# The second block's mixer: the values' and the latents' projections moved between the rounds of neighbourhood attention

## The reference

```
z = rms_norm(h, mix_pre_g) @ w_in                 # 512 x 1952
q_na, k_na, v_na, c_q, c_kv, k_rope = split(z)    # 512, 512, 512, 256, 128, 32 columns
o_na  = neighbourhood_attention(q_na, k_na, v_na, na_rpb)
o_mla = latent_attention(c_q, c_kv, k_rope, q_norm_g, w_uq, kv_norm_g, w_ukv, cos, sin)
mixed = concat(rms_norm(o_na), rms_norm(o_mla)) @ w_out
h = h + rms_norm(mixed, mix_post_g)
```

## Time and profile before

| | us |
|---|---|
| median of 3 runs | 1896.31 (1894.67 to 1901.78) |
| the profiled execution, its own time | 1902.84 |
| its span, first to last instruction | 1901.0 |
| TensorE busy | 1801.5 (95%) |
| VectorE busy | 962.7 (51%) |
| ScalarE busy | 853.9 (45%) |
| mean granted TensorE clock | 0.972 |

### The profile page before, as it was taken

How to read it: one execution, slowest core, us unless ns; L and a number is a source line. 1 busy time by engine, 2 the same in 40 slices (tenths; PEclk the granted TensorE clock), 3 DMA queues, 4 the chain that set the end, 5 groups by cost and what they waited for, 6 DMA issues and landing times.

```text
span 1901.0 us, 22849 instructions
## 1 busy us (share of the span) xinstructions
PE 1801.5 (95%) x8653; PEld 1424.6 (75%) x8653; DVE 962.7 (51%) x1528; ACT 853.9 (45%) x1336; POOL 261.1 (14%) x317
## 2 busy tenths in 40 slices
PE   8998999999779999989999999998899999999997
PEld 6886666667658888867888888776577678888886
DVE  3546344445369999965432343443656453323334
ACT  4236665552348888864222322323555442222222
POOL 4001532220001111120000000160223100000000
PEclk9998999999979999999999999999799999999998
DMA  7224011114469999673332333143101223223321
GB/s 212 86 73 133 24 41 49 45 45 155 177 257 359 385 384 388 260 239 106 92 107 81 108 91 109 60 137 91 51 12 54 58 78 99 100 88 101 98 101 56
DMA packets 161172, 246.59 MB, mean 130 GB/s; under 512 B 11346, under 2 KB 117041, under 8 KB 148144
## 3 DMA queue, kind: packets, MB, share of 16 engines
q1 hardware_dynamic: 152768, 232.57, 36.3%
q0 software_dynamic: 8304, 12.69, 2.2%
HBM read 239.42 MB, written 12.61 MB: 133 GB/s over the span
## 4 chain that ended last, share of the span: by engine, by line
PE 88%; DVE 6%; ACT 3%; issue 2%; DMA 1%; POOL 0%; DVEq 0%; SPq 0%; ACTq 0%
PE psum L472 25%; PE psum L474 25%; PE psum L473 24%; PE psum L624 3%; PE psum L652 3%; PE psum L608 3%; ACT warea_r L432 1%; PE psum L630 1%; PE psum L1353 1%; DVE xarea L2041 1%; DVE warea_r L438 1%; DVE xarea L2412 1%; DMA arena<-in_w_in 0%; ACT arena L1706 0%; DMA arena<-y_assigned 0%
## 5 line engine op out<-in xcount | busy, mean ns | idle before, releaser
L438 DVE TENSOR_TENSOR warea_r<-warea,warea_r 128x2048 fp32r<-128x2048 f32 x108 | 250.7, 2322 | 318.5 <-ACT warea_r L432 318.4
L472 PE MATMUL psum<-tarea_r,warea_r 128*128 128x512 f32 x916 | 366.0, 400 | 4.0 <-DVE tarea_r L2051 3.8
L474 PE MATMUL psum<-tarea_r,warea_r 128*128 128x512 f32 x916 | 359.1, 392 | 0.0
L473 PE MATMUL psum<-tarea_r,warea_r 128*128 128x512 f32 x916 | 359.0, 392 | 0.0
L472 PE MATMUL psum<-warea_r,arena_r 128*128 128x512 f32 (+1 forms) x768 | 300.3, 391 | 12.9 <-DVE warea_r L438 4.0
L432 ACT ACTIVATE warea_r<-warea 128x2048 fp32r<-128x2048 f32 x108 | 205.9, 1907 | 234.4 <-PE psum L474 231.9
L474 PE MATMUL psum<-warea_r,arena_r 128*128 128x512 f32 (+1 forms) x768 | 297.5, 387 | 0.0
L473 PE MATMUL psum<-warea_r,arena_r 128*128 128x512 f32 (+1 forms) x768 | 297.2, 387 | 0.0
L472 PEld LDWEIGHTS psum<-tarea_r,warea_r 128*128 128x128 f32 x916 | 173.2, 189 | 48.3 <-issue 10.0
L474 PEld LDWEIGHTS psum<-tarea_r,warea_r 128*128 128x128 f32 x916 | 173.3, 189 | 36.9
L473 PEld LDWEIGHTS psum<-tarea_r,warea_r 128*128 128x128 f32 x916 | 173.4, 189 | 34.7 <-issue 0.7
(11 more groups left out here) (329 smaller groups left out, 2465.8 us busy)
## 6 DMA issues: line engine op xcount, KB each, us to landing
warea<-in_ffn_w_gu SPq DMA_DIRECT2D x88, 512.0 KB, 5.0
warea<-in_w_in SPq DMA_DIRECT2D x40, 512.0 KB, 4.5
warea<-in_ffn_w_down SPq DMA_DIRECT2D x40, 512.0 KB, 4.2
arena<-in_w_up SPq DMA_DIRECT2D x16, 1024.0 KB, 7.4
tarea<-in_w_up SPq DMA_DIRECT2D x16, 1024.0 KB, 7.3
tarea<-in_w_down SPq DMA_DIRECT2D x16, 1024.0 KB, 7.7
warea<-in_w_gate SPq DMA_DIRECT2D x14, 1024.0 KB, 7.4
harea<-in_w_gate SPq DMA_DIRECT2D x14, 1024.0 KB, 7.9
```

Of the source, the lines that this page charges most:

```text
L438: dve.tensor_tensor(w_lo[:, u % 2, :], raw_of(u), w_hi[:, u % 2, :].bitcast(f32), ALU.subtract)\
L472: nc.tensor.matmul(out, high, by_high, start=first, stop=False)
L473: nc.tensor.matmul(out, high, by_low, start=False, stop=False)
L474: return nc.tensor.matmul(out, low, by_high, start=False, stop=last)
```

## The change

- Tables 0, 1 and 2 are made between the halves of the keys' block, into banks 0 to 2. Table 3 comes at the end of TensorE's round 0, tables 4 to 7 at the ends of rounds 6, 7, 9 and 10 (on VectorE at the starts of rounds 1, 7, 8, 10 and 11).
- The values' block is no longer ahead of the rounds: its first half is fill of rounds 0 (row blocks 0, 1) and 1 (2, 3), its second half of rounds 2 and 3, in banks 6, 4, 7, 5. The evacuations are in ScalarE's openings of rounds 3 and 4.
- The latents' block is fill of rounds 4 to 7 (row blocks 0 and 1 by halves, then 2, then 3), with evacuations in rounds 6 to 8.
- The splits of units 5, 6 and 7 move into the closings (ScalarE: 6 in round 1, 7 in round 3; VectorE: 0, 2 and 4). Pair 0's evacuation, unit 8's high part and the root are all in ScalarE's closing of round 8; VectorE's variance, evacuation and rotation in 8, unit 8's low part in 9, scaling in 9 and 10, the copy and unit 9's low part in 11.
- Turning in rounds 11 and 12, MLA jobs in 13 to 20, sums of squares in 21. The band transfers stand one unit earlier in SyncE's queue.

The diff, cut:

```diff
 MLA_AT = 4 * NT
+TABLE_ROUND = {1: (3,), 7: (4,), 8: (5,), 10: (6,), 11: (7,)}
...
 
+        if ph["name"] == "second":
+            yield from TABLE_ROUND.get(d, ())
...
-            if u is not None and ph["units"][u]["last_of_pair"]:
...
-        return [j for j in (2 * (d - 12), 2 * (d - 12) + 1) if 0 <= j < len(MLA_JOBS)]
...
             for u in range(AT_MID, AT_FFN2):
                 feed(u)
-                if u == AT_MID + 9:
+                if u == AT_MID + 8:
                     sp.wait_ge(s["z2_evac"], 4)
                     for b, band in enumerate((0, 8, 24, 32)):
                         for r in range(4):
                             src = v2[64 * (r % 2) + band:64 * (r % 2) + band + 32, :, :]
                             sp.dma_start(Vband[32 * r:32 * r + 32, b, :].rearrange("p (j n) -> p j n", j=2),
                                          src[:, r // 2:r // 2 + 3:2, :]).then_inc(s["band_in"], 16)
...
-            for n in range(3):
+            for n in range(2):
...
-                    if n == 2 and h == 0:
+                    if n == 1 and h == 0:
                         pe.wait_ge(s["xrev_in"], 16 * 8 * H)
+                        for g in range(3):
+                            pe.wait_ge(s["z2_first"], g + 1)
+                            na_table(g, ps[g])
+            pe.wait_ge(s["na_tab"], 3)
+            pe.wait_ge(s["z2_first"], 5)
+            def values(r, h):
+
+                u = AT_MID + 4 + h
                 if r == 0:
-                    for h in range(2):
-                        pe.wait_ge(s["split_lo"], AT_MID + 6 + h + 1)
-                else:
-                    pe.wait_ge(s["z2_evac"], 4 + r)
-                for k in range(KD):
-                    mm = products(ps[6][:, 0:416], hT_hi[:, k, P * r:P * r + P], hT_lo[:, k, P * r:P * r + P],
-                                  *weights(AT_MID + 6 + k // 4, 416 * (k % 4), 416), k == 0, k == KD - 1)
-                mm.then_inc(s["z2_psum"], 1)
+                    pe.wait_ge(s["split_lo"], u + 1)
+                if h == 0:
+                    if r < 2:
+                        pe.wait_ge(s["z2_first"], (7, 5)[r])
+                    else:
+                        pe.wait_ge(s["na_tab"], 4)
+                for c in range(4):
+                    k = 4 * h + c
+                    mm = products(ps[V_BANK[r]], hT_hi[:, k, P * r:P * r + P], hT_lo[:, k, P * r:P * r + P],
+                                  *weights(u, 512 * c, 512), k == 0, k == KD - 1)
+                if h:
+                    mm.then_inc(s["z2_psum"], 1)
+                elif r == NT - 1:
+                    mm.then_inc(s["unit_done"], 1)
+
+            def latent(r, h):
+
+                u = AT_MID + 6 + h
+                if r == 0:
+                    pe.wait_ge(s["split_lo"], u + 1)
+                if h == 0:
+                    pe.wait_ge(s["z2_evac"], (1, 3, 5, 7)[r])
+                for c in range(4):
+                    k = 4 * h + c
+                    mm = products(ps[7 if r == 1 else 6][:, 0:416], hT_hi[:, k, P * r:P * r + P], hT_lo[:, k, P * r:P * r + P],
+                                  *weights(u, 416 * c, 416), k == 0, k == KD - 1)
+                if h:
+                    mm.then_inc(s["z2_psum"], 1)
 
...
+                pe.wait_ge(s["cn_ready"], 5 if c == 3 else 4)
                 if c < 2:
-                    pe.wait_ge(s["cn_ready"], 5)
...
             def second_fill(d):
 
-                if 1 <= d <= 4:
-                    if d == 1:
-                        pe.wait_ge(s["na_tab"], 1)
-                    latent(d - 1)
-                if d in (10, 11):
-                    latent_turned(2 * (d - 10))
-                    latent_turned(2 * (d - 10) + 1)
+                if d < 4:
+                    for r in range(2 * (d % 2), 2 * (d % 2) + 2):
+                        values(r, d // 2)
+                for r, h in {4: ((0, 0), (1, 0)), 5: ((0, 1), (1, 1)), 6: ((2, 0), (2, 1)), 7: ((3, 0), (3, 1))}.get(d, ()):
+                    latent(r, h)
+                for g in tables_at(second, d + 1):
+                    if g == 3:
+                        pe.wait_ge(s["z2_first"], 8)
+                    if g == 4:
+                        pe.wait_ge(s["z2_evac"], 6)
+                    na_table(g)
+                if d in (11, 12):
+                    latent_turned(2 * (d - 11))
+                    latent_turned(2 * (d - 11) + 1)
                 for j in mla_jobs(d):
                     mla_job(j)
-                if d == 20:
+                if d == 21:
                     pe.wait_ge(*mla_evac(len(MLA_JOBS) - 1))
                     pe.wait_ge(*mla_evac(len(MLA_JOBS) - 2))
                     norm_sums(0)
                 if d in OUT_ROUND:
                     out_job(OUT_ROUND[d])
 
-            attend_pe(pe, second, na_table, second_fill)
+            attend_pe(pe, second, fill=second_fill)
...
-            for n in range(3):
+            for n in range(2):
                 split_high(AT_MID + 2 * n + 2)
                 if n == 0:
                     row_copy(3, ps[7])
-                for r in range(4 if n > 1 else 0):
-                    q = 4 * n + r
-                    act.wait_ge(s["z2_psum"], q + 1)
-                    nc.scalar.activation(v2[:, r, :], ps[q % 8], ACT.Identity, scale=late[3][:, r:r + 1]).then_inc(s["z2_evac"], 1)
                 split_high(AT_MID + 2 * n + 3)
 
             def second_opening(d):
 
-                if 2 <= d < 6:
-                    r = d - 2
+                for r in {3: (0, 1), 4: (2, 3)}.get(d, ()):
+                    act.wait_ge(s["z2_psum"], 8 + r + 1)
+                    nc.scalar.activation(v2[:, r, :], ps[V_BANK[r]], ACT.Identity, scale=late[3][:, r:r + 1])\
+                        .then_inc(s["z2_evac"], 1)
+                for r in {6: (0, 1), 7: (2,), 8: (3,)}.get(d, ()):
                     act.wait_ge(s["z2_psum"], 12 + r + 1)
-                    nc.scalar.activation(z3[:, r, :], ps[6][:, 0:416], ACT.Identity, scale=late[3][:, r:r + 1])\
+                    nc.scalar.activation(z3[:, r, :], ps[7 if r == 1 else 6][:, 0:416], ACT.Identity, scale=late[3][:, r:r + 1])\
                         .then_inc(s["z2_evac"], 1)
-                for c in {11: (0, 1), 12: (2, 3)}.get(d, ()):
+                for c in {12: (0, 1), 13: (2, 3)}.get(d, ()):
                     act.wait_ge(s["cn_psum"], c + 1)
                     nc.scalar.activation(krot if c == 3 else cT_hi[:, c, :], ps[6 + c % 2], ACT.Copy).then_inc(s["ct_ready"], 1)
                 for j in mla_jobs(d - 1):
...
             def second_closing(d):
 
-                if d == 5:
+                if d == 1:
+                    split_high(AT_MID + 6)
+                if d == 3:
+                    split_high(AT_MID + 7)
+                if d == 8:
+                    evac_high(0)
                     latent_high(AT_MID + 8, Q_PARTS)
-                if d == 6:
                     root(rstd[:, 16:24])
-                if d == 7:
+                if d == 10:
                     latent_high(AT_MID + 9, KV_PARTS)
-                if d == 21:
+                if d == 22:
                     root(rstd[:, 24:28])
-                if d in (20, 22, 27, 33):
-                    split_high(AT_MID + {20: 10, 22: 11, 27: 12, 33: 13}[d])
-
-            attend_act(act, second, pair_high(second, lambda pair: o2[pair // 4][0][:, pair % 4, :], 984),
-                       fill=second_opening, split=second_closing)
+                if d in (20, 23, 27, 33):
+                    split_high(AT_MID + {20: 10, 23: 11, 27: 12, 33: 13}[d])
+
+            evac_high = pair_high(second, lambda pair: o2[pair // 4][0][:, pair % 4, :], 984)
+            attend_act(act, second, evac_high, fill=second_opening, split=second_closing)
...
             for n in range(2):
                 split_low(AT_MID + 2 * n + 2)
                 if n == 0:
                     dve.wait_ge(s["row_ready"], 3)
+                else:
+                    dve.wait_ge(s["const_in"], 32)
+                    for g in range(3):
+                        na_table(g, ps[g])
                 for r in range(4):
...
-                split_low(AT_MID + 2 * n + 3)
-            split_low(AT_MID + 6)
-            split_low(AT_MID + 7)
+                if n == 0:
+                    split_low(AT_MID + 3)
...
-                for c in {11: (0, 1), 12: (2,)}.get(d, ()):
+                for c in {12: (0, 1), 13: (2,)}.get(d, ()):
...
             def second_closing(d):
 
-                if 2 <= d < 6:
-                    t = d - 2
+                for u in {0: (5,), 2: (6,), 4: (7,)}.get(d, ()):
+                    split_low(AT_MID + u)
+                for t in {6: (0, 1), 7: (2,), 8: (3,)}.get(d, ()):
                     dve.wait_ge(s["z2_evac"], 4 + t + 1)
                     for k, (a, b_) in enumerate(((0, 256), (256, 384))):
```

(46 more changed lines are left out.)

35 lines of the change are left out of this document (5 added, 30 removed).

## The result

The changed kernel took 1908.36 us (median of 6 runs, 1904.90 to 1913.62) against 1898.53 for the kernel before (6 runs, 1894.67 to 1901.78): ratio 1.0054 [1.0037, 1.0071]. It is slower by half a per cent, 12 us over the forecast of 1896 and outside its range. The profiled execution took 1906.38 with a span of 1904.5, 3.5 more than the span before; the stretch from round 22 to the end is 474.4 in both, so the difference arises ahead of it, as the prediction had it.

A forecast was written before the change was run, and what follows sets the result against it. It held TensorE to bound the stretch only while a projection lies beside the rounds, the VectorE-ScalarE loop bounding rounds 5 to 12. The gap's gain was given back at later waits: minus 0.1 us, so 1896, range 1886 to 1902.

The forecast's parts named there:

- Step 1: Keys' block: three tables add 1.9 us of TensorE; VectorE has time for its nine operations, 3.1 us.
- K: End of the keys' products, forecast at 1285.4 (1283.49 + 1.9); later times in the prediction are counted from it.
- Steps 2 to 5: Rounds 0 to 12: old gap gone, round 8 7.8 us earlier, then given back at waits; first MLA job at 91.4.
- Step 6: First MLA job to round 22: 49.7 us against 51.9 before, by minus 1.16 and minus 1.0; moved sums of squares nothing.
- The sum: Whole kernel: minus 0.1 us, span 1901.0 to 1900.9, median 1896.2, rounded 1896.
- A: First output product, round 5: no wait for the band transfers; minus 6 us, 1890; 15%.
- B: Rounds 8 to 12 run at 4.94 us each despite ScalarE's block; first job 6.1 earlier, 1890; 15%.
- C: TensorE's clock stays at half through rounds 13 and 14 after three gaps; plus 4.1 us, 1900; 15%.
- D: Rounds 0 to 3: each round's values wait and are not fill, showing as idle time; 2%, inside C's chance.
- that I don't see: An unnamed wait that, together with C, would make the kernel slower by 9.5 us; 6%.
- The rule weighed: ScalarE's table switches, end of round 8: skill's 2.66 each would give 1899; the forecast kept 1.30.

The follow-up runs named there:

- e1: Changed kernel with table 2 no longer waiting on TensorE for tables 0 and 1: 1898.10 us, ratio 0.9999 to the kernel before.
- e4: The changed kernel run again unaltered, as base of its group: 1906.42 us, ratio 1.0034 to the kernel before.
- e2: Kernel before with only tables 0 and 1 moved between the halves of the keys' block: 1897.45 us, ratio 0.9988.
- e7: e1 with value rows evacuated before the split, plus e5's and e6's edits and tables 6 and 7 a round earlier: 1893.82 us, ratio 0.9982.
- e10: e1 with value rows 2 and 3 evacuated before the split, plus the edits of e5 and e6: 1894.34 us, ratio 0.9968.
- e6: e1 with value rows evacuated before the split, and unit 8's high part moved to round 8's opening: 1892.93 us, ratio 0.9961.
- e9: Changed kernel, wait kept, with five idle matmuls (ten in the trace) before table 2: 1904.59 us, ratio 1.0027 to the kernel before.
- e5: e1 with value rows evacuated before the split, and GpSimd issuing half of the band transfers: 1894.82 us, ratio 0.9978.

## Why the prediction was wrong

**Step 1 failed.** All that made the stage longer than forecast lies in it. It priced three tables by their matmuls, 3 x 0.65 = 1.9, and asked only whether VectorE's nine operations would delay the keys' evacuation. It did not ask what `na_table` waits for: for table 2, the tables 0 and 1 as VectorE has them, and in VectorE's queue these stand behind the low part of a unit whose split begins when the keys' first half ends. The terms were in the rows: a split of 1.9 and table operations of 2.07 for six, a low part of 2.3 by the profile's page. Together 6.3; TensorE's own tables 0 and 1 fill 1.3 of it (2 x 0.65), so the wait would have come out at 5.0. I had even named VectorE's queue as the cause of the old gap, from the earlier trace rows, and did not carry that reading to the new place: the old gap's line of waits said what the moved call depends on. K was to be 24.56 after the row factor (1283.49 + 1.9 - 1260.83); without the wait it was 24.73 (e1), with it 31.48 and, in the second trace, 32.84. "Nothing" as the lower bound and 3.1 as the upper one were bounds of the wrong queue: VectorE's delay, not TensorE's wait.

**Steps 2 to 5 held,** counted from the first scores, 1291.19: first output product at 1335.11 behind a wait of 4.85 (I had 4.05) and at half clock for 3.31 (3.8); round 8 at +60.4 (59.4); second output product +68.9 (68.1; the forecast start of its idle time and its length gave the same place); table 7 +79.6 (79.5) behind 6.17 (6); first MLA job +91.4 (91.4). The last one is in part luck: the terms from 88.0 on, at most a bare round of 1.63, 0.6 and 0.65, add up to 90.9 and not to the 91.4 that I wrote. The band's transfers took 11.41 of SyncE, 0.85 more than in the earlier trace rows, and that is the longer wait.

**Step 6** was 2.1 long: from the first job to round 22 it is 47.6, not 49.7. The first twelve products of the jobs went at full clock; I had taken 1.0 for that, half of the clock's cost, and it was 1.8 (4.70 before, 2.94 now). The other 1.2 is the term that I put at nothing, what runs at half clock behind the sums of squares. Round 21 took 8.16 in the trace of the kernel before and 6.95 in that of e2, which has the same instructions there. One us in the scores of that round, before and then in e2:

```profile
1420.00:1421.00 1.00, 1.00 (x8) 0.84 (x6) 0.00 (x0) 1.00 (x2) 0.19 (x1) 0.50 0.00 0
```
```profile
1416.00:1417.00 1.00, 1.00 (x12) 0.91 (x10) 0.00 (x0) 1.00 (x2) 0.20 (x1) 1.00 0.00 0
```

The changed kernel had 1.00 from 1423 to 1429, over its sums and what follows them. So 1.2 of the 51.9 that I started from belonged to the one trace rather than to the program, as far as two traces tell, and that it made the stage's miss smaller is luck.

**The sum.** Step 1 cost 6.9 more than I had (31.48 less 24.56), the rest 2.2 less (138.9 from the first scores to round 22 against 141.1), so the stage would be 4.7 over my forecast, and the first traces show 4.6 over the stage before. The medians show more: 12.0 over the 1896.31 that the forecast started from. Of this, 2.2 is the median of the kernel before (1896.31 in three runs, 1898.53 in six), which leaves 9.8. Without the 1.2 of round 21 the two traces of the changed kernel are 5.8 and 8.1 over the stage before, and the second group of runs has the medians 6.8 apart (1906.42 in e4, 1899.64 before). What of the 9.8 lies beyond that is not shown; the runs scatter ahead of the stage by more.

**The rivals.** A (no wait for the band) fell with the 4.85; B (rounds 8 to 12 at 4.94 each) with round 13 at 1380.29, 28.7 behind round 8; C (clock at half through rounds 13 and 14) with 1.00 from 1383 on; D spoke of rounds 0 to 3, which are full. The cause was in none of them: it was the wait that I gave 6% together with C as one "that I don't see".

**The rule weighed.** ScalarE's timeline of the changed kernel, where the root is (the counterpart of the earlier trace rows):

```profile
1355.82 2.18 ACT L456 ACTIVATE warea_r<-warea 128x1024 fp32r<-128x1024 f32 x4
1358.02 1.28 ACT L1674 ACT_TABLE_LOAD   x1
1359.31 0.21 ACT L1674 ACTIVATE rstd<-rstd 128x8 f32<-128x8 f32 x1
1359.43 0.64 ACT L730 ACTIVATE harea<-psum 128x256 f32<-128x256 f32 x2
1360.08 1.28 ACT L740 ACT_TABLE_LOAD   x1
1361.38 0.51 ACT L740 ACTIVATE garea<-garea,nmax 128x256 f32<-128x256 f32 x1
```

The next instruction starts 1.29 and 1.30 after the start of the load. The Trainium skill, ScalarE: Activation LUTs, section "What ACT_TABLE_LOAD costs", would have 2.66; the measurement decides, and the place was forecast rightly with 1.30.

## What to carry to other kernels

When a call of a helper moves, take the row that names its present wait as the first price of its new place, read the waits inside the helper, above all those that hang on an index, and walk each back through the queue of the engine that releases it in its new place: a wait that was free at the end of a block can cost a split, a low part and the work itself in the middle of one. Filling a gap on the main engine moves its cost to the next place that has to wait for the others; before doing it, price the smallest part alone, which here (two tables moved) was worth as much as the whole once that was free of its wait. Where a mended kernel has several waits of 2 to 6 us on one loop of two other engines, taking them away one by one need not add up: the three of e7 did not, the two of e10 did by stage.

## What was not expected of the hardware

- After the wait of 5.18 the granted clock was 0.50 in the us at 1278 and 0.53 in the one at 1280, 1.00 from 1281; in the second trace of the same program (e4) it was 0.50 for some 5.6 us behind the same wait. After waits of 3.85 to 4.85 the output product took 3.28 to 3.68, after 2.07 and less 1.97, after 2.39 (e6) 3.22, after 2.19 2.78 (e6) and 3.46 (e10). The clock cost up to 1.7 us at an output product, and 1.4 and 2.7 us behind the wait in the keys' block.
- The same instructions of round 21 ran at 0.50 in the trace of the kernel before and at 1.00 in that of e2: 8.16 against 6.95 us.
- The same program's stage differed by 2.3 us between two traces, and what lies ahead of the stage by over 10: the row factor's matmul started between 1252.51 (e1) and 1265.87 (e6), though nothing before it was changed.
- Sixteen transfers of 128 KB took SyncE 10.39 (e9) to 11.41 (changed kernel) to issue, and eight of them beside GpSimd's eight 8.16 to 8.88 (e7, e5, e10).
